# A two-layer hybrid decoder step on one core: the tokens in two parts per layer, with the mixer steps of one part between the dense weight jobs of the other

## What is computed

```python
def _layer(h, p_l, lst, w, lb, pos, wbuf, prompt):
    u = _rmsnorm(h, w['norm1_g']) @ w['w_in']                  # 1024 x 3080
    (a_x, a_g, b_q, b_k, b_v, c_q, c_f, c_i, c_g,
     d_q, d_k, d_v, d_o, d_i, d_f) = jnp.split(u, SPLIT_IDX, axis=-1)
    y_a, h_new, conv_new = _rglru(a_x, a_g, ...)               # RG-LRU: causal conv, gates, linear scan
    q, k = _rope(_rmsnorm(b_q)), _rope(_rmsnorm(b_k))
    y_b = _swa_prompt(q, k, v, w['attn_sinks'])                # window 128, with sinks (sample: its cache)
    y_c, s_new = _hgrn2(c_q, c_f, c_i, c_g, lb, s0, ...)       # gated linear attention in chunks
    y_d, c_new, n_new, m_new = _mlstm(d_q, d_k, d_v, d_o, d_i, d_f, ...)   # mLSTM in chunks
    h = h + jnp.concatenate([y_a, y_b, y_c, y_d], axis=-1) @ w['w_out']
    f = _rmsnorm(h, w['norm2_g']) @ w['w_up']                  # 1024 x 4096
    h = h + jnp.square(jax.nn.relu(f)) @ w['w_down']           # 4096 x 1024
    h = h + jax.nn.sigmoid(h @ w['w_ple_gate']) * (p_l @ w['w_ple_proj'])
    return h, states
```

## Time and profile before

| what | value |
|---|---|
| median of three runs | 3230.73 us (3230.63 to 3238.65) |
| profiled execution, span from first to last instruction | 3234.4 us |
| mean granted TensorE clock | 0.935 of full speed |
| TensorE busy | 2971.1 us, 92% |
| VectorE, ScalarE, GpSimd busy | 36%, 28%, 28% |
| mean DMA rate | 48 GB/s |

### The profile page before, as it was taken

One profiled execution on the slowest core, in us unless ns is written; L12 is line 12 of the kernel. 1 busy time (PEld: TensorE's weight loads), 2 busy tenths in 40 slices (PEclk: granted clock), 3 DMA queues, 4 the chain that ended last, 5 costly groups with the idle time before them and its releaser, 6 DMA issues.

```text
span 3234.4 us, 43899 instructions
## 1 busy us (share of the span) xinstructions
PE 2971.1 (92%) x18128; PEld 2801.4 (87%) x18128; DVE 1149.4 (36%) x2022; ACT 905.8 (28%) x1377; POOL 905.2 (28%) x591
## 2 busy tenths in 40 slices
PE   5988977889999999999968899778899999999999
PEld 4887865579999999999967788655899999999998
DVE  4643255553222222222355423566422222222223
ACT  4443222233111111113345332223331111111133
POOL 2111244222222332225131112432122223222251
PEclk8999976789999999999979999768899999999999
DMA  4010100021111111112210111000211111111112
GB/s 165 33 48 27 59 20 7 9 88 40 49 50 45 45 45 49 42 46 69 79 59 23 46 41 58 14 1 9 94 44 49 46 45 45 49 48 45 63 52 79
DMA packets 42756, 155.78 MB, mean 48 GB/s; under 512 B 6786, under 2 KB 8066, under 8 KB 41088
## 3 DMA queue, kind: packets, MB, share of 16 engines
q1 hardware_dynamic: 33696, 125.68, 11.3%
q10 hardware_dynamic: 8928, 28.28, 2.3%
HBM read 136.18 MB, written 17.76 MB: 48 GB/s over the span
## 4 chain that ended last, share of the span: by engine, by line
PE 81%; DVE 11%; ACT 3%; issue 3%; POOL 2%; DMA 0%; ACTq 0%; DVEq 0%; SPq 0%; POOLq 0%
PE pj L338 24%; PE pj L339 24%; PE pj L340 24%; DVE small L1648 2%; DVE ext L1334 2%; DVE ext L1843 1%; PE pm L351 1%; DVE small L1334 1%; PE pj L579 1%; DVE vt L1334 1%; PE pm L545 1%; PE pm L430 1%; POOL w_lo L1190 1%; PE pm L549 1%; PE pm L531 1%
## 5 line engine op out<-in xcount | busy, mean ns | idle before, releaser
L338 PE MATMUL pj<-m_hi,w_hi 128*128 128x344 f32 x1920 | 614.4, 320 | 0.0
L340 PE MATMUL pj<-m_hi,w_lo 128*128 128x344 f32 x1920 | 613.2, 319 | 0.0
L339 PE MATMUL pj<-m_lo,w_hi 128*128 128x344 f32 x1920 | 612.7, 319 | 0.0
L338 PE MATMUL pj<-n_hi,w_hi 128*128 128x344 f32 x1584 | 526.5, 332 | 71.9 <-DVE n_lo L1334 27.5
L340 PE MATMUL pj<-n_hi,w_lo 128*128 128x344 f32 x1584 | 516.1, 326 | 0.0
L339 PE MATMUL pj<-n_lo,w_hi 128*128 128x344 f32 x1584 | 516.0, 326 | 0.0
L339 PE MATMUL pj<-hid_lo,w_hi 128*128 128x344 f32 x1536 | 492.9, 321 | 0.0
L338 PE MATMUL pj<-hid_hi,w_hi 128*128 128x344 f32 x1536 | 490.8, 320 | 0.0
L340 PE MATMUL pj<-hid_hi,w_lo 128*128 128x344 f32 x1536 | 490.2, 319 | 0.0
L1243 POOL TENSOR_TENSOR w_lo<-w_raw,w_hi 128x1024 fp32r<-128x1024 f32 x128 | 308.4, 2409 | 628.6 <-ACT w_hi L1082 628.6
L1190 POOL TENSOR_TENSOR w_lo<-w_raw,w_hi 128x1024 fp32r<-128x1024 f32 x84 | 212.1, 2526 | 827.4 <-ACT w_hi L735 827.4
(11 more groups left out here) (330 smaller groups left out, 3430.5 us busy)
## 6 DMA issues: line engine op xcount, KB each, us to landing
w_raw<-in_w SPq DMA_DIRECT2D x216, 512.0 KB, 3.2
out_y<-res ACTq DMA_DIRECT2D x16, 516.0 KB, 2.7
res<-out_y ACTq DMA_DIRECT2D x2, 3096.0 KB, 11.2
res<-in_x SPq DMA_DIRECT2D x4, 1032.0 KB, 8.0
out_y<-res SPq DMA_DIRECT2D x8, 516.0 KB, 15.8
ext<-in_rope SPq DMA_DIRECT2D x2, 1032.0 KB, 12.5
res<-out_y ACTq DMA_DIRECT2D x2, 1032.0 KB, 4.9
hsq<-in_p ACTq DMA_DIRECT2D x2, 1032.0 KB, 4.7
```

The lines of the kernel that those rows point to most:

```text
L338: pe.matmul(pj[:, t, 0:TT], wh, hi[:, k, cols], start=(k == 0), stop=False)
L339: pe.matmul(pj[:, t, 0:TT], wh, lo[:, k, cols], start=False, stop=False)
L340: last = pe.matmul(pj[:, t, 0:TT], wl, hi[:, k, cols], start=False, stop=(k == nk - 1))
```

## The change

The tokens are taken in two parts: part 0 holds the first 512 prompt tokens, as one token tile of 512; part 1 the other 512 and the 8 sample tokens, as two tiles of 260. Each layer is done for part 0 and then for part 1; an *instance* i = 0, 1, 2, 3 is a pair of part and layer (i % 2 and i // 2). Each instance has its own 107 weight jobs, 428 in all, of 24 matmuls with 512 columns or 48 with 260; the weights are loaded and split for each. The states that pass from part 0 to part 1 stay in SBUF. The loops over layers and feed-forward steps are written out.

`_order` now lists the dense work in stages, and `slot_steps` puts mixer steps behind jobs: at most one step that has work on TensorE, and one without. The mixer of instance 0 stands among the w_in jobs of instances 0 and 1; that of instance 1 from the end of w_in of instance 1 on, among the w_out and feed-forward jobs of instance 0; those of instances 2 and 3 likewise. HGRN2's chunk is split into `h0` (differences, exponentials, products: no TensorE), `h1` (scores) and `h2` (outputs, state), the mLSTM's into `m1` and `m2`. The 8 `m_lo` of instances 1 and 2 are made one after the other (`mf`), just ahead of a feed-forward.

There are three weight buffers instead of two (`NW`), and the low part overwrites `w_raw`. Three PSUM banks (`NB`) are a ring over all token tiles, norms, gates and rotations.

```diff
-TT = T // 3
+HALF = SEQ // 2
+NCH = HALF // CH
+WMAX = HALF + DEC
+INST = 2 * LAYERS
+PART = ((0, HALF, ((0, HALF),)),
+        (HALF, WMAX, ((0, WMAX // 2), (WMAX // 2, WMAX))))
...
+NB = 3
+NW = 3
...
+def _mixer(i):
...
+    o += [('h0', 0, 'cq1'), ('h1', 0, 'cq1')]
+    for c in range(NCH):
+        if c + 1 < NCH:
+            o += [('h0', c + 1, 'cq1')]
+        o += [('h2', c, 'cq1')]
+        if c + 1 < NCH:
+            o += [('h1', c + 1, 'cq1')]
...
+    stages = [
+        squares(0) + norm(0),
+        between(win[0], squares(1) + norm(1), 1, 2),
+        win[1],
+        out[0] + ffn[0][:1] + [('n2', 0, 0), ('xl', 1, 0)] + ffn[0][1:] + ple[0],
+        out[1][:1] + [('n1', 2, 0)] + between(out[1][1:], [('nf', 2, k) for k in range(KT)], 0, 2),
+        win[2][:1] + [('n2', 1, 0)] + win[2][1:] + [('mf', 1, k) for k in range(KT)],
+        ffn[1] + ple[1],
+        out[2][:1] + [('n1', 3, 0)] + between(out[2][1:], [('nf', 3, k) for k in range(KT)], 0, 2),
+        win[3][:1] + [('n2', 2, 0)] + win[3][1:] + [('mf', 2, k) for k in range(KT)],
+        ffn[2] + ple[2],
+        out[3] + ffn[3][:1] + [('n2', 3, 0)] + ffn[3][1:] + ple[3],
+    ]
...
+    def slot_steps(gap):
+        heavy = light = False
+        while queue:
+            i, (step, arg, need) = queue[0]
+            at = ready.get((i, JOB[need]))
+            if at is None or count - at < gap:
+                return
+            if light or (heavy and not _light(step, arg)):
+                return
+            light, heavy = _light(step, arg), True
+            order.append((step, i, arg))
+            queue.pop(0)
...
+            def unit(what, i, a, n, k0, nk, hi, lo, ready=None):
+                for t, (c0, c1) in tiles(i):
+                    key = (what, i, a, t)
+                    free(key)
+                    for k in range(nk):
+                        if ready and t == 0:
+                            ready(k)
+                        last = passes(pj[:, bank(key), 0:c1 - c0], n, slice((k0 + k) * P, (k0 + k + 1) * P),
+                                      hi(k), lo(k), k, nk, slice(c0, c1))
+                    last.then_inc(mm[bank(key)], 1)
```

More of the change, by code:

```diff
@@ L68 @@
     N_SO += _s
-def _order():
[L73 to L88, removed]
@@ new lines, in job, with reload, gate @@
+            def job(what, i, a):
+                n = JOBS[(what, i, a)]
+                if n + NW < len(JOB_LIST):
+                    g = JOB_END[n]
+                    sp.wait_ge(mm[g % NB], g // NB + 1)
+                    weights(n + NW)
+            def reload(i, _):
+                if i == 0:
+                    sp.wait_ge(mc_h, NCH)
+                    sp.wait_ge(gd_v, 2)
+                else:
+                    full(sp, ('out', 0, KT - 1, 0))
+                stream(i)
+            def gate(i, _):
+                if i == 1:
+                    for n in range(4):
+                        for t, _ in tiles(i):
+                            full(sp, ('gate', i, n, t))
+                    sp.dma_start(wrwi[:], wrwi_in[1]).then_inc(wr_ld, 16)
@@ new lines, in _ @@
+            stream(0)
+            sp.dma_start(cst[:], consts).then_inc(cst_ld, 16)
+            for l in range(LAYERS):
+                sp.dma_start(par[:, l, :], par_in[l]).then_inc(cst_ld, 16)
+            weights(0)
+            weights(1)
+            stream(1)
+            weights(2)
+            sp.dma_start(wrwi[:], wrwi_in[0]).then_inc(wr_ld, 16)
+            for what, i, a in ORDER:
+                if (what, i, a) in JOBS:
+                    job(what, i, a)
+                elif what == 'xl':
+                    reload(i, a)
+                elif what == 'gate':
+                    gate(i, a)
@@ new lines, in msample @@
+                    last.then_inc(ms_t, 1)
+                elif part == 1:
+                    pe.wait_ge(ms_p, l + 1)
+                    pe.wait_ge(mc_h, gi(i, NCH))
+                    for n in range(2):
+                        last = pe.matmul(pm[:, 3 + n, :], blk, smp_half(n, 15), start=True, stop=True)
+                    last.then_inc(ms_pt, 1)
+            steps = dict(win=win, out=out, up=up, down=down, proj=proj, pg=pg, n1=n1, n2=n2, vt=vtrans, rowt=rowt,
+                         gate=gate, rope=rope, attn=attn, sattn=sattn, hdiag=hdiag, hsample=hsample, h1=h1, h2=h2,
+                         hnorm=hnorm, mnorm=mnorm, mprep=mprep, m1=m1, m2=m2, msample=msample)
@@ L726, in _ @@
+            for what, i, a in ORDER:
+                if what in steps:
+                    steps[what](i, a)
         @block.scalar
@@ L1329, in _ @@
+            for what, i, a in ORDER:
+                if what == 'nf' and not started:
+                    split_lo(0)
+                    started = True
+                if what == 'win' and (i, a) == (0, 0):
+                    split_lo(1)
+                if what in ('win', 'out', 'pg'):
+                    split_lo(JOBS[(what, i, a)] + 2)
+                elif what in steps:
+                    steps[what](i, a)
         @block.vector
@@ L1883, in _tiles @@
+            link(dve.memset(q_diag[:], 0.0))
+            for what, i, a in ORDER:
+                if what in steps:
+                    steps[what](i, a)
 def _tiles(w, k0, n):
```

2955 lines of the change are left out of this document (1504 added, 1451 removed).

## The result

The changed kernel takes 3256.29 us (median of 4 runs, 3251.4 to 3259.08) against 3234.69 us of the kernel before: a ratio of 1.0065, 95% interval 1.0049 to 1.008. It is slower by 0.65%; the forecast was 3033 us, and faster. The profiled execution has a span of 3249.6 us.

What follows compares the result with a forecast made beforehand. TensorE, busy 92% of the span, was taken to bound the kernel, with time to give only in mixer stretches. A floor of 2833 us plus 204 us of waits made 3037, predicted as 3033 us; range 2915 to 3145.

Steps and rivals of the forecast that it cites:

- the floor: Whole kernel: dense matmuls 2414, mixer and norm matmuls 384, start 30 and end 5 us make 2833 us.
- rival 1: Dense matmuls: 260 columns take the 156.7 ns of 344, 360 us on top, 3393 us; chance 0.06.
- Weights loaded and split twice: Weight jobs: 428 splits instead of 215, GpSimd gains 520 us of work; cost in dense stretches 0.
- resource left open: VectorE and GpSimd hold each other up on SBUF operands; the change doubles the splits; not in the sum.
- rival 3: HGRN and mLSTM chunks: GpSimd's splits also lie on VectorE's chain, 78 and 19 us, 3130 us; chance 0.20.
- Sample-token steps: Mixers' sample tokens: 18 steps wait between 0 and one 1.84 us transposition, 0.9 each, 16 us.
- Every mixer step now stands behind a job of the other part: Mixer stretches: each step's wait is covered by one dense job, 5.6 us on average.
- rival 2: Mixer stretches: jobs and steps don't overlap in in-order queues with three banks, 294 us of waiting stay, 3140 us; chance 0.10.
- HGRN: 19.8 us per chunk: HGRN chunk: chain of 14.9 us plus two weight splits, 2.5 us short of cover, 16 chunks, 40 us.
- m_lo, 17 us: Low parts of two norms, eight at a time before an up job: 10 to 20 us, 17 taken.
- theory A: Follow-up theory on mixer stretches: a step's chain outlasts its one job, and next jobs' banks are taken behind it; about 300 us.
- Each switch to and from a mixer step: TensorE at 64 chunk steps: two switches each at 0.25 us of issue time, 32 us.

Runs made afterwards that it cites:

- short split: Against the changed kernel: GpSimd subtracts 8 columns instead of 1024 per job, the third pass multiplies by the high part; 3120.1 us.
- two banks: Two PSUM banks instead of three, against the changed kernel with two jobs behind long mixer steps and cache loads at the first attention step: 3298.5 us.
- spread steps: Against the changed kernel: ten kinds of longer mixer steps in instances 1 to 3 get two dense jobs instead of one; 3197.7 us.
- split h0: h0 gets its own place behind the job after h1, against the changed kernel with two jobs behind long steps and early cache loads: 3126.8 us.
- caches, cover and split length mended: Against the changed kernel: early cache loads, two jobs behind longer mixer steps, and 8-column weight subtraction without the low part; 3048.8 us.

## Why the prediction was wrong

- *What bounds the kernel, and the floor.* Right. Dense matmuls cost 119.6 and 230.4 ns, where 121.7 and 226.7 were taken; rival 1 (157 ns for 260 columns), the only one slower than the kernel before, did not happen. The mixers' 384 us, at full clock, did not hold as well: dense and mixer matmuls together are busy 121 us longer than the floor has them. The first dense matmul starts at 22.7 us, where 30 us were allowed.
- *"Weights loaded and split twice ... Cost in the dense stretches: 0, covered by the jobs themselves."* This is the step that failed, by what it left out. In the dense stretches the 0 is right (TensorE is busy for all of the 50 us of both windows). In the mixer stretches the splits were priced only as 2 x 2.44 us in GpSimd's queue of an HGRN chunk. The hold on VectorE was seen in the earlier trace rows, named as a resource left open, and put into a rival (rival 3, 3130 us) with a chance of 0.20. Without the splits' length 136 us go, where that rival had 97. The chunks are not alone in paying: the longest norm addition falls from 2.88 to 0.70 us with the short split, the longest m_lo from 2.39 to 0.76, the longest row scan (L1843) from 2.57 to 1.48.
- *"Sample-token steps: 18, each between 0 and one 1.84 us transposition."* 16 us were taken, the two waits for the cache load alone are worth 50. The bounds counted instructions and left the DMA out: its place in the program had moved to the end of attention, one job ahead of its use, and the load takes 25.7 us. The trace of before has no wait for it, which was no price for its new place.
- *"Every mixer step now stands behind a job of the other part, 5.6 us on average."* The cover was counted for TensorE's next mixer matmul. It was not asked who takes the job's bank: VectorE, behind 13 us of the same mixer step, with three banks in between. This is rival 2's queue argument (17 waits for VectorE's additions with three banks, 38 with two); two banks, spread steps and the split h0 show it, with +138, -59 and -34 us. Rival 2's time, 3140 us, is 116 us short of the result: it kept the waiting of before, and idle time grew.
- *HGRN: 19.8 us per chunk.* 22.6 to 29.4 were measured. The chain of 14.9 us in the kernel before ran in three groups of levels, matmuls of one beside products of the next:

```profile
469.80 0.58 DVE L1334 TENSOR_TENSOR ext<-small,res 64x128 f32<-64x128 f32 x2
469.83 1.16 PE L531 MATMUL pm<-ext,vt 128*128 128x128 f32 x8 [1.69 <-DVE ext L1334]
470.40 0.59 DVE L1334 TENSOR_TENSOR ext<-par,res 64x128 f32<-64x128 f32 x2
```

The change makes `h1` and `h0` one after the other with single buffers, and that was in the code and not in the sum. No run with a second set of buffers gives its price.
- *m_lo, 17 us:* Half as large, and by luck near a number of the trace. TensorE's three waits behind L1540 add up to 17.8 us, but they are these:

```profile
540.92 0.79 PE L563 MATMUL pj<-xop_r,w_hi 128*128 128x512 f32 x1 [9.14 <-DVE xop_r L1540]
1383.16 0.56 PE L563 MATMUL pj<-xop_r,w_hi 128*128 128x260 f32 x1 [6.45 <-DVE xop_r L1540]
2211.29 0.47 PE L563 MATMUL pj<-xop_r,w_hi 128*128 128x512 f32 x1 [2.20 <-DVE xop_r L1540]
```

  The second and third are the two heaps, 8.7 us together. The first is a single m_lo of instance 0, which is in no heap: it stands behind 11 us of RG-LRU steps in VectorE's queue, which is theory A again.
- *"Each switch to and from a mixer step ...: 32 us."* The 0.21 and 0.33 us of the earlier trace rows are idle time of the weight loads (PEld), not of the matmuls. The matmul rows of the changed kernel show no gap at such a switch: L815 is listed to 751.61 us (ends of matmuls are modelled), and the next dense matmul has started at 751.37.
- *The sum as a whole.* With caches, cover and split length mended it is 214 us over the floor, where the forecast had 204. With a switch term that no matmul row shows, an m_lo term twice too large and an HGRN term too small, that is luck in part, and no proof of the terms.

So of the 223 us between forecast and result, 207 go with three edits whose causes the sum did not hold: a late load, splits that hold VectorE, and too little cover for steps that stand in the way of the banks. The third edit adds cover and does not take the cause away. How the 136 us of the splits divide exactly between the hold and GpSimd's own queue stays open; the waits that GpSimd ends give 18 us to the second.

## What to carry to other kernels

In this kernel, work that was moved beside other work was paid for in the engines' queues, not in their busy shares: for each step that is put between jobs, ask who takes the job's results and what stands before it there. Where two parts need the same weights twice, count every engine's preparation of them at the place where it will stand. A transfer that moves with a step needs its own cover; where the trace of before shows no wait for it, that says nothing about its new place.

## What the runs showed of the hardware

A GpSimd instruction on SBUF keeps VectorE's operations on two SBUF tiles waiting until it ends: single products of 0.28 us at the shortest took up to 2.40 us beside splits of 2.42 us, and 0.74 at most, as without splits, beside pieces of 0.78. Selections that read PSUM kept a median of 446 and a maximum of 752 ns. The Trainium skill, "SBUF — State Buffer", section "SBUF: two separate sides", states such an exclusive lock for the whole instruction, and the trace agrees. Its size in this kernel: 186 us of VectorE's 1292.8; 136 us of the time went with the splits' length, GpSimd's own queue included.

In dense stretches at a granted clock of 1.00, what a matmul costs above its columns at 2.4 GHz is not constant: 11.3 ns at 260 columns (119.6 - 108.3), 13.4 at 344, 17.1 at 512 (230.4 - 213.3).

Two cache loads of 508 KB each, issued 0.6 us apart, landed 25.7 us after the second was issued; a weight load of 512 KB takes 3.3 us in the median. Why they take so long was not tried.
